# Two gate multiplications of a state-space mixer moved from VectorE to GpSimd

## The reference

```python
def hybrid_mixer(u, p, i):
    proj = u @ p["w_in"][i]
    ...
    h_fwd, h_bwd = hyena_filters(L, ...)              # sin network, output layer fw3, decay window
    z = (v * x1).astype(f32)
    z = bidir_long_conv(z, h_fwd, h_bwd) + z * p["hy_bias"][i].astype(f32)
    y_hy = rmsnorm(x0.astype(f32) * z, p["hy_norm"][i])
    gate = proj[..., o1:o2]
    ...
    y_ssm = y_f + y_b + xs.astype(f32) * p["ssm_D"][i].astype(f32)[:, None]
    y_ssm = rmsnorm(y_ssm.reshape(b, L, SSM_WIDTH) * jax.nn.silu(gate.astype(f32)), p["ssm_norm"][i])
    y = jnp.concatenate([y_hy, y_ssm], axis=-1).astype(u.dtype)
    return y @ p["w_out"][i]
```

## Time and profile before

| | us |
|---|---|
| median of 3 runs | 2335.8 |
| lowest, highest | 2334.77, 2337.49 |
| the profiled execution: its time | 2337.58 |
| the profiled execution: its span | 2334.8 |
| TensorE busy in the span | 2306.0 (99%) |
| VectorE busy | 1456.0 (62%) |
| ScalarE busy | 1143.5 (49%) |
| GpSimd busy | 389.4 (17%) |

### The profile page before, as it was taken

One profiled execution on the slowest core, in us unless ns is written; L12 is line 12 of the kernel. 1 busy time (PEld: TensorE's weight loads), 2 busy tenths in 40 slices (PEclk: granted clock), 3 DMA queues, 4 the chain that ended last, 5 costly groups with the idle time before them and its releaser, 6 DMA issues. The chain is left out here.

```text
span 2334.8 us, 32848 instructions
## 1 busy us (share of the span) xinstructions
PE 2306.0 (99%) x12624; PEld 2154.4 (92%) x12624; DVE 1456.0 (62%) x2287; ACT 1143.5 (49%) x2248; POOL 389.4 (17%) x448
## 2 busy tenths in 40 slices
PE   8999999999999999999999999999999999999998
PEld 7999679898999999999989985998989999999987
DVE  8887784476575454636478878736756846354454
ACT  5554445555554353536445535445455534444362
POOL 1121002200112121212111110023002121212120
PEclk9999999999999999999999999999999999999999
DMA  5554327842456555665555553288216465656563
GB/s 162 114 110 103 91 86 166 182 104 60 91 113 129 133 120 125 128 139 116 114 119 110 108 122 91 70 178 181 77 46 132 98 132 126 128 121 133 119 153 88
DMA packets 111288, 275.27 MB, mean 118 GB/s; under 512 B 12630, under 2 KB 13910, under 8 KB 111140
## 3 DMA queue, kind: packets, MB, share of 16 engines
q0 software_dynamic: 63936, 116.42, 30.0%
q1 hardware_dynamic: 47204, 156.84, 22.4%
HBM read 270.06 MB, written 3.15 MB: 117 GB/s over the span
## 5 line engine op out<-in xcount | busy, mean ns | idle before, releaser
L567 POOL DMA_DIRECT2D wlo<-wstream x332 | 291.9, 880 | 1346.8 <-ACT wlo L600 1127.8
L600 ACT ACTIVATE wlo<-raw 128x512 fp32r<-128x512 f32 x292 | 183.6, 629 | 509.0 <-PE G L1203 429.1
L1203 PE MATMUL G<-B_hi,whi 128*128 128x384 f32 x1120 | 375.1, 335 | 0.0
L1203 PE MATMUL G<-B_hi,wlo 128*128 128x384 f32 x1120 | 374.2, 334 | 0.0
L1203 PE MATMUL G<-B_lo,whi 128*128 128x384 f32 x1120 | 374.1, 334 | 0.0
L1203 PE MATMUL G<-A_hi,whi 128*128 128x384 f32 x864 | 294.8, 341 | 9.6 <-DVE A_lo L1855 8.1
L1203 PE MATMUL G<-A_hi,wlo 128*128 128x384 f32 x864 | 290.7, 336 | 0.0
L1203 PE MATMUL G<-A_lo,whi 128*128 128x384 f32 x864 | 285.9, 337 | 0.0
L1823 DVE TENSOR_TENSOR scaled_out<-G,rbc 128x768 f32<-128x768 f32 x56 | 53.6, 958 | 276.8 <-PE G L1203 252.5
L1203 PEld LDWEIGHTS G<-B_hi,whi 128*128 128x128 f32 x1120 | 210.2, 188 | 0.8 <-issue 0.7
L1203 PEld LDWEIGHTS G<-B_lo,whi 128*128 128x128 f32 x1120 | 210.2, 188 | 0.5 <-issue 0.5
(11 more groups left out here) (485 smaller groups left out, 4994.3 us busy)
## 6 DMA issues: line engine op xcount, KB each, us to landing
raw<-wstream SPq DMA_DIRECT2D x220, 512.0 KB, 4.0
wlo<-wstream POOLq DMA_DIRECT2D x332, 256.0 KB, 5.3
w_low<-wstream POOLq DMA_DIRECT2D x96, 256.0 KB, 4.1
raw_b<-wstream SPq DMA_DIRECT2D x32, 512.0 KB, 5.9
ring<-dft SPq DMA_DIRECT2D x8, 512.0 KB, 4.0
mraw<-memT SPq DMA_DIRECT2D x16, 256.0 KB, 3.2
X<-xT SPq DMA_DIRECT2D x8, 384.0 KB, 6.0
win<-dft SPq DMA_DIRECT2D x6, 512.0 KB, 4.7
```

Of the source, the lines that this page charges most:

```text
L567: pool.dma_start(low, wstream[stream(L, c)][:, part], accum_op=ALU.add).then_inc(lo_in[c % 2][h], 16)
L600: act.activation(wlo[:, s, part], raw[:, s, part], ACT.Copy, scale=-1.0).then_inc(neg_done, 1)
L1203: last = mm(out, w, p[:, k, a:b], start=(k == 0 and w is w_hi and p is parts[0]), stop=(k == KT - 1 and (w is w_lo and only is None or onl ...
```

## The change

For the last two token tiles (4 and 5) the multiplication by the gate goes from VectorE's list to GpSimd's. GpSimd does it right behind the two transfers of chunk 25, after it has waited for `off_add` to reach the layer's last value and for the tile's gate. It raises a semaphore of its own, `yg_p`, and ScalarE's `square_y` waits for that one where the tile is 4 or 5. VectorE keeps the tiles 0 to 3. This holds in both layers. Shapes, types and the arithmetic are the same.

```diff
@@ -370,6 +370,7 @@
+        yg_p = sem("yg_p")
@@ -570,6 +571,11 @@
             for L in range(DEPTH):
                 for c in range(0 if L else AHEAD, C_MLP):
                     low_halves(L, c)
+                    if c == C_GATE + 3 + AHEAD:
+                        pool.wait_ge(off_add, L * 8 + 8)
+                        for t in (4, 5):
+                            pool.wait_ge(gate_ev, L * TT + (t + 1))
+                            pool.tensor_tensor(ysum[:, t, :], ysum[:, t, :], gate[:, t, :], ALU.mult).then_inc(yg_p, 1)
@@ -773,7 +779,7 @@
                 def square_y(t):
-                    act.wait_ge(yg_r, L * TT + t + 1)
+                    act.wait_ge(*((yg_r, L * 4 + t + 1) if t < 4 else (yg_p, L * 2 + t - 3)))
                     act.activation(gate[:, t, :], ysum[:, t, :], ACT.Square,
                                    accum_out=stat[:, 2, t:t + 1]).then_inc(yg_s, 1)
@@ -2119,8 +2125,9 @@
                     ins.then_inc(f_h, 1)
-                    dve.wait_ge(gate_ev, L * TT + (i + 1))
-                    tt(ysum[:, i, :], ysum[:, i, :], gate[:, i, :], ALU.mult).then_inc(yg_r, 1)
+                    if i < 4:
+                        dve.wait_ge(gate_ev, L * TT + (i + 1))
+                        tt(ysum[:, i, :], ysum[:, i, :], gate[:, i, :], ALU.mult).then_inc(yg_r, 1)
```

## The result

The changed kernel is slower, by 0.3%. In the first comparison it took 2344.85 us in the median of 15 runs (2336.68 to 2354.76) against 2337.18 for the kernel before: the ratio is 1.0031, 95% interval [1.0024, 1.0038]. The forecast was -1.9 us and the range ended at 2337.9. The runs of the changed kernel also spread over 18 us, where those of the kernel before lie within 4 but for one disturbed run.

What follows compares the result with a forecast made beforehand. TensorE, busy 99% of the span, was taken to bound the kernel. Removing its wait before `filter_dft` gained 0.95 us per layer, what is added cost nothing: 2335.8 - 1.9 = 2333.9 us, range 2331.8 to 2337.9.

Steps and rivals of the forecast that it cites:

- What the change removes: Two multiplications leave VectorE's chain of folds, so TensorE's wait before `filter_dft` goes: -0.95 us per layer, -1.9 in all.
- TensorE's idling priced at its own length: An edit on another engine costs only the time it makes TensorE, busy for 99% of the span, stand still.
- what is added: Two GpSimd multiplications and two waits per layer, plus one `ISA` instruction in the first layer: no cost in the forecast.
- the hold-up: GpSimd's multiplications hold VectorE instructions that read two SBUF tiles: 2334.4 to 2337.7 us, in between 2336.0; chance 0.24.
- the rival's upper end: Hold-up late in the first layer, early in the second, 1.23 us per multiplication: -1.9 + 2.46 + 1.38 = +1.9, 2337.7 us.
- 2d - 1.08: Per-layer loss if both multiplications (d each) precede VectorE's gapless chain, less its 1.08 us waits: 0.26 at d=0.67, 1.38 at 1.23.
- its sign: TensorE's wait before `z_dft` grows past 0.41 us, with VectorE's two-SBUF-input rows longer than 0.67 to 0.69.
- the rival's low end: Hold-up early in both layers at 0.67 us per multiplication: -1.9 + 0.52 = -1.4, 2334.4 us.
- The ISA instruction: Unnamed GpSimd instruction ahead of the first layer's multiplications, perhaps fetching code: taken as 4.1 us, upper end 10.5.
- the deadline of the squares: VectorE's line 2132 needs ScalarE's six squares; `ISA` instruction plus two multiplications must stay below 11.6 us, 5.4 expected.
- x: Time of the `ISA` instruction before GpSimd's multiplications, first layer only: 4.1 us taken, 10.5 the upper end.
- The rival of the late code: First layer: the `ISA` instruction's code fetch makes VectorE wait at line 2132 amid its folds; +8.6 us, 2344.4; chance 0.05.

Runs made afterwards that it cites:

- removed: The changed kernel with GpSimd's two multiplications left out, so token tiles 4 and 5 are never multiplied; 2333.33 us against 2334.79 for the kernel before.
- dve_delay3: The kernel before plus three unused VectorE additions per layer ahead of the first-row mend, nothing added on GpSimd; 2336.85 us against 2335.09.
- dve_delay: The kernel before plus four unused VectorE additions per layer ahead of the first-row mend, nothing added on GpSimd; 2344.41 us against 2335.15.
- experiment 11: The changed kernel run and profiled once more without any edit; 2339.69 us against 2335.09 for the kernel before, ratio 1.0020.
- pool_copy: The kernel before plus two unused 128x512 GpSimd copies, reading one SBUF tile each, at the place of the change; 2335.49 us against 2335.15.
- after_fill: The changed kernel with TensorE repeating token tile 4's four transposes four times ahead of the third filter product's wait; 2336.60 us against 2334.79 for the kernel before.
- pool_extra: The kernel before, nothing removed from VectorE, plus two unused GpSimd multiplications at the place of the change; 2344.59 us against 2335.15.
- pool_early: The changed kernel with GpSimd multiplying before chunk 25's transfers, after the fifth of eight additions; 2333.07 us against 2334.79 for the kernel before.
- after_one: The changed kernel with only token tile 5 multiplied on GpSimd and tile 4 back on VectorE; 2335.80 us against 2335.09 for the kernel before.
- pool_memset: The kernel before plus two 128x1536 GpSimd memsets, which read nothing, at the place of the change; 2335.29 us against 2335.15.

## Why the prediction was wrong

*What the change removes: right.* -0.95 us per layer was the step; `removed` shows 0.90 between the same two rows, and the two versions without a hold on the path gain 1.7 us against the 1.9 forecast.

*The step that failed: TensorE's idling priced at its own length.* The prediction's first paragraph says that an edit on another engine "costs only what it makes TensorE stand still", and the forecast put what is added at nothing, with the hold-up as a rival. The hold-up came, and by itself it would have stayed inside the range: it turns the -1.9 us into +1.7, and the rival's upper end was +1.9. Of the 7.7 us by which the first comparison's medians differ, the other 6.0 are no wait but slow matmuls: TensorE stands still for 1.45 and 1.38 us, and its granted clock is 0.50 for about 17 and 14 us behind them. The clock is in no term and in no rival. `dve_delay3` and `dve_delay` show that an idle stretch of 0.8 us costs its length here and one of 1.5 us can cost several us more, by experiment 11 some 6 to 8. Experiments 4, 6 and 11 tie it to the idling: filled, the fall is gone; made on VectorE alone, it is there; and it comes in some executions and layers and not in others, with the wait the same. The Trainium skill ("TensorE: Matmul & The Clock Gate", Part 1) says that TensorE's clock has a half and a full level, set by how busy it has lately been, and that where the transition falls varies from run to run; the trace agrees with its 0.50 and 1.00 and with the two groups of times. Why one execution falls and another doesn't was not tested. In the four profiled executions with the long wait the second layer fell each time and the first only once.

*The rival of the mutual hold-up: the right mechanism, too short a length, the wrong path, and a price that comes out by luck.* I took 0.67 us for one multiplication, with 1.23 as the upper end. It is 1.28 alone, and two in a row hold the mend for 2.84 us. The Trainium skill's figure ("GPSIMD Engine Reference", Performance versus the Vector engine; the prediction's estimate from it is about 1.1 us) was nearer than the row that I used. The rival's price was "2d - 1.08", counting VectorE's two waits as spare time, and its sign was a longer wait before `z_dft`. But the instruction that is held is the mend of the first tile, and TensorE waits for that one too, in front of its third product. There the spare time was 1.27 us, as two rows of the kernel before show, VectorE's mend and TensorE's third product:

```profile
265.39 0.68 DVE L2115 TENSOR_TENSOR hpa<-hpa 1x512 f32<-1x512 f32 x1
```

```profile
267.34 1.02 PE L1407 MATMUL G<-rmem_bc,acc 66*128 66x512 f32 x2
```

The mend ends at 266.07, the product starts at 267.34. No row that the prediction uses has this distance, since it did not bind; I looked only for waits that the profile lists, not for those just below. 2.84 us of hold against 1.27 of slack makes 1.6 us of lateness of TensorE itself. VectorE uses up its two waits as the rival had it, but TensorE's late products set the rest: the fifth tile starts at 275.31 in `after_again`, right behind its product and 1.73 us late. The wait before `z_dft` stays at 0.41. With the measured hold the rival's formula gives 2.84 - 1.08 = 1.76 us, and `z_dft` is 1.74 late: nearly the right number, because two different slacks are of nearly the same size. Net of the gain the hold costs +0.84 us per layer, where the rival's low end had a gain. What the wrong path hid is the new idle stretch of TensorE, and with it the clock.

*The ISA instruction and the deadline of the squares: right, and beside the point.* The first multiplication starts at 265.96, before the row of the last transfer ends (265.31 + 0.86), so x is about nothing. ScalarE squares tiles 4 and 5 directly behind tile 3, long before line 2139 runs. The rival of the late code, which I made the slower side, does not exist here. That its time, 2344.4, lies near the first median is chance.

*The rule on the shared port: right on the reads, not on who comes first.* The Trainium skill ("SBUF — State Buffer", Who interferes with whom) has it that a VectorE instruction with two SBUF inputs contends with GpSimd instructions that read, not with those that only write, and the runs agree: multiplications +2.84 us, copies +1.40, memsets 0.00, and line 2116 with its one SBUF input unchanged. It also has it that whichever starts first keeps the port. By the rows the mend started first (265.81 against 265.96) and was held through both multiplications, though the second starts 1.23 us behind the first; the measurement decides, as far as a row's start says when the port is asked for. It may not say it: the mend ends 0.55 us behind GpSimd's last row whether its own row starts 0.15 us ahead of GpSimd's first or 0.04 (265.40 + 3.52 against 265.55 + 2.82 in `after_again`, 266.26 + 2.08 against 266.30 + 1.49 in `pool_copy`).

## What to carry to other kernels

Before moving work to another engine, look up not only who waits for the work but which instructions will run beside it, and for each of these the time until its consumer would start to wait, though no wait is listed yet. On a TensorE that is busy 99% of the time, a new idle stretch of over a microsecond may cost several times its length through the clock (here up to 7.8 us for 1.5); where one can't be avoided, matmuls without use can be cheaper than standing still, as in `after_fill`. And when a chain is too long, look first for an idle stretch of the same engine earlier on: moving two instructions up gave the same gain as a second engine at its best.

## What the runs showed of the hardware

- Two multiplications of 128x512 f32 in a row on GpSimd start 1.23 us apart (265.81 and 267.04 in `pool_extra`) and have rows of 1.60 us each beside a held VectorE instruction; in `pool_early`, with no hold on them, the rows are 1.28 and 1.29. A copy of the same size is 0.95, a memset of 128x1536 1.72.
- A VectorE instruction of one partition and 512 elements, 0.68 us by itself, is held for 2.84 us by them. The hold reaches over the boundary between two GpSimd instructions.
- GpSimd's multiplication, too, is 0.3 us longer beside the mend than in `pool_early`, a single one as well (1.61 in `after_one`). What it waits for was not tested.
- In the filter stage the granted clock fell only behind the idle stretches of 1.4 to 1.5 us, and in part of the cases (two layers of two in the first profile of the changed kernel; the second layer alone in its second, in `pool_extra` and in `dve_delay`). It did not fall behind one of 0.8, neither in the profile nor, by the mean clock, in any of 11 runs. It returned after some 13 to 17 us of unbroken work at half speed.
- An idle stretch is not all there is to it. In `pool_memset` TensorE idles 1.51 us before 24.86, and the clock reads 1.00 after it. In the kernel before it is at 0.50 from 1219 to about 1222 us, though TensorE lists no wait from 1200 us on and is busy throughout. Such a fall of about 3 us stands in several of the profiles, mostly near 65 us; no run explains it.
